# Two-layer hybrid backbone on one core: modulation slices in another order, and the first two feature tiles projected side by side

## The chip, the cores and the metric

The kernel runs on one NeuronCore of a Trainium2 chip. The metric is the device time of one execution in microseconds (us); less is better. All the work is float32 or float32 split into two parts, and the engines run side by side, held together by semaphores that are written out by hand.

## What is computed

Two layers work on 512 latent and 256 context tokens (768 columns here) of width 1024. In each layer a normed and modulated token matrix is projected, four branches mix the tokens, a gated sum is projected back, and a gated feed-forward part follows. Only the first lines of the first layer matter here:

```python
mod_l = (jax.nn.silu(c) @ w_mod[l] + b_mod[l])[:, None, :]
mod_c = (jax.nn.silu(c_ctx) @ w_mod[l] + b_mod[l])[None, None, :]
sh1, sc1, g1, sh2, sc2, g2 = jnp.split(mod_l, 6, axis=-1)
...
hl = modulate(rms_norm(x, norm1[l]), sh1, sc1)
hc = modulate(rms_norm(xc, norm1[l]), sh1c, sc1c)
y_l, y_c = token_mixer(hl, hc, w_in[l], ...)     # zl = split_cols(hl @ w_in), zc = split_cols(hc @ w_in)
```

`modulate(h, shift, scale)` is `h * (1 + scale) + shift`.

## The kernel before

**Operand tiles.** The modulated matrix is held turned, as 8 tiles of 128 features by 768 tokens. Each is split into a leading part `hh` (ScalarE, L1508) and a rest `hl` (VectorE, L1998); weights are split in the same way into `w_hi` and `w_lo` by GpSimd (L1342, L1345). A product is then three matmuls (L517 to L519).

**Modulation.** `w_mod` of the first layer comes as slices of 256 by 512 (`msl`, group g, quarter kk). Group 0 and 1 are the two halves of the shift `sh1`, group 2 and 3 those of the scale `sc1`; groups 4 to 11 are for later. PE multiplies each slice by the conditioning (L614). When a group's four slices are done, ScalarE copies the sum out (`modulation_columns`, L1475), PE turns it (`modulation_turned`, L623) and ScalarE adds the bias (`modulation_bias`, L1480). VectorE makes the factor `a1` of the norm from groups 2 and 3 (L1904). Between the slices PE turns the 8 tiles of normed tokens (`turn_tokens("xn", k)`, L998), which ScalarE (even k, L1417) and VectorE (odd k, L1855) copy to SBUF. Before, the groups come in the order 0, 1, 2, 3, and all 8 operand tiles are made after the last of them.

**The raw tokens.** While the first feature tile is projected, PE also turns the raw tokens (`turn_tokens("x", n)` inside `product`), and ScalarE copies each to `xT` (`tokens_again`, L1417), over the normed tile that has been read by then.

**Feature tiles.** The retention branch has four feature tiles, here called f0 to f3, then two pairs of token tiles. Each feature tile is 8 steps of the contraction by 768 columns, in a run of 512 and one of 256 columns for each half of the contraction. f0 uses PSUM banks 0 and 1, f1 banks 2 and 3, f2 banks 0 and 1 again. The modulation groups 0 to 3 use banks 0 to 3, group 4 uses bank 7, and the turned tokens use banks 4 to 7.

**The ring.** All weights come through a ring of four slots of 512 KB, in the order of `weight_chunks`, on SP's DMA queue. A chunk is issued only when the chunk four places ahead of it has been used (a `msl` slice: by PE; a feature tile: when both halves have been split by GpSimd). Counted from 0, the 16 slices of groups 0 to 3 have the places 0 to 15. Before, f0 has place 16, slices 4.0 and 4.1 have 17 and 18, f1 19, slices 4.2 and 4.3 20 and 21, f2 22, slices 5.0 and 5.1 23 and 24, and f3 25. The tables `dist` and `rope` are issued on the same queue, behind f0 and behind f1.

## Time and profile before

| | us |
|---|---|
| median of 3 runs | 2730.15 |
| lowest and highest of them | 2726.96 and 2737.42 |
| the profiled execution | 2744.37 |
| its span, first to last instruction | 2742.6 |
| PE busy in it | 2596.0 (95%) |
| VectorE, ScalarE, GpSimd busy | 1354.9, 714.2, 1472.9 |

The span is what the instructions cover; 1.8 us of the profiled execution lie around it. The profiled execution took 14.2 us more than the median of the runs, so a step that is read from the trace is worth the same microseconds, but is taken from another total. Busy shares are means over the whole: the first 2% of the span, which the change touches, look quite different from the rest.

### The profile page before, as it was taken

To read this page: it belongs to the slowest core of one execution; us is meant where nothing else is said; L and a number is where in the kernel's file an instruction comes from. 1 tells how busy PE (TensorE), PEld (TensorE's weight loads), DVE (VectorE), ACT (ScalarE), POOL (GpSimd) and SP (SyncE) were. 2 spreads that over 40 slices of the span, in tenths; PEclk is the share of its full clock that TensorE was granted. 3 is DMA by queue.
4 is the path that set the end of the run, shared out by engine and by line. 5 is a ranking of instruction groups with operands and counts; after the bars stand their busy time and mean duration, and the time that the engine had idled before them with its cause. 6 is when DMAs were issued, how large, how long until landed. Compare 5 with 4: busy or idle time off the path is not lost.

```text
span 2742.6 us, 37892 instructions
## 1 busy us (share of the span) xinstructions
PE 2596.0 (95%) x15444; PEld 2141.7 (78%) x15444; DVE 1354.9 (49%) x1877; ACT 714.2 (26%) x1216; POOL 1472.9 (54%) x1375
## 2 busy tenths in 40 slices
PE   5999999998998999999999999998999889999999
PEld 2788887877876888888878888796777667888877
DVE  3522256543466867555574463326653767512231
ACT  4411333222254621111120121133331455211110
POOL 2533547522423436666669435546733436588886
PEclk8999999999999999999999999999999999999999
DMA  7422412311311844444433462312221227433322
GB/s 266 146 72 73 141 43 68 87 43 57 105 42 58 267 122 126 122 121 122 121 102 112 127 215 67 86 51 69 74 62 43 62 74 245 116 100 93 98 85 79
DMA packets 378210, 285.23 MB, mean 104 GB/s; under 512 B 10309, under 2 KB 338729, under 8 KB 377526
## 3 DMA queue, kind: packets, MB, share of 16 engines
q1 hardware_dynamic: 375744, 279.94, 34.2%
q8 instruction: 123, 2.02, 0.3%
q10 hardware_dynamic: 1686, 2.78, 0.3%
q14 instruction: 49, 0.40, 0.0%
q0 software_dynamic: 608, 0.09, 0.0%
HBM read 253.42 MB, written 29.36 MB: 103 GB/s over the span
## 4 chain that ended last, share of the span: by engine, by line
PE 80%; DVE 10%; POOL 3%; ACT 3%; issue 2%; DMA 1%; ACTq 0%; SPq 0%; DVEq 0%; POOLq 0%
PE ps L517 18%; PE ps L518 17%; PE ps L519 17%; PE ps L1191 3%; PE ps L723 3%; PE ps L561 2%; PE ps L563 2%; PE ps L562 2%; DVE ffl L2421 2%; PE ps L807 2%; PE ps L827 1%; POOL w_lo L1345 1%; PE ps L932 1%; POOL w_hi L1342 1%; PE ps L1140 1%
## 5 line engine op out<-in xcount | busy, mean ns | idle before, releaser
L1342 POOL TENSOR_TENSOR w_hi<-ring,tiny 128x512 fp32r<-128x512 f32 x480 | 537.5, 1120 | 1037.8 <-PE ps L519 626.9
L517 PE MATMUL ps<-hh,w_hi 128*128 128x512 f32 (+1 forms) x2320 | 848.4, 366 | 15.8 <-DVE hl L1998 9.5
L1345 POOL TENSOR_TENSOR w_lo<-ring,w_hi 128x512 fp32r<-128x512 f32 (+1 forms) x568 | 796.1, 1404 | 98.3 <-ACT w_hi L1546 60.3
L518 PE MATMUL ps<-hl,w_hi 128*128 128x512 f32 (+1 forms) x2320 | 823.7, 355 | 0.0
L519 PE MATMUL ps<-hh,w_lo 128*128 128x512 f32 (+1 forms) x2320 | 822.7, 355 | 0.0
L517 PEld LDWEIGHTS ps<-hh,w_hi 128*128 128x128 f32 x2320 | 444.6, 192 | 112.2 <-issue 27.2
L519 PEld LDWEIGHTS ps<-hh,w_lo 128*128 128x128 f32 x2320 | 444.5, 192 | 61.9
L518 PEld LDWEIGHTS ps<-hl,w_hi 128*128 128x128 f32 x2320 | 445.0, 192 | 58.5 <-issue 2.4
L1644 ACT ACTIVATE arena<-ps,tiny,vec 128x768 f32<-128x768 f32 (+1 forms) x120 | 108.7, 906 | 192.4 <-DVE tiny L2156 185.9
L2430 DVE SCALAR_TENSOR_TENSOR arena<-ps,vec,arena 128x511 f32<-128x511 f32 x66 | 43.6, 660 | 219.8 <-ACT arena L1810 219.0
L517 PE MATMUL ps<-ffh,w_hi 128*128 128x512 f32 x352 | 139.7, 397 | 12.8 <-DVE ffl L2421 11.4
L1810 ACT ACTIVATE arena<-ps,vec 128x768 f32<-128x768 f32 (+1 forms) x44 | 39.1, 888 | 424.5 <-PE ps L519 424.5
L1921 DVE SCALAR_TENSOR_TENSOR rope<-ring,tiny,rope 128x1024 f32<-128x1024 f32 x84 | 146.0, 1779 | 0.9
L519 PE MATMUL ps<-ffh,w_lo 128*128 128x512 f32 x352 | 137.2, 390 | 0.0
L518 PE MATMUL ps<-ffl,w_hi 128*128 128x512 f32 x352 | 137.1, 390 | 0.0
L561 PE MATMUL ps<-w_hi,hh 128*128 128x256 f32 x448 | 131.6, 294 | 3.7 <-POOL w_lo L1345 2.7
L1526 ACT ACTIVATE arena<-ps 128x512 f32<-128x512 f32 (+3 forms) x118 | 66.8, 568 | 249.6 <-PE ps L519 246.1
L563 PE MATMUL ps<-w_hi,hl 128*128 128x256 f32 x448 | 128.5, 287 | 0.0
L562 PE MATMUL ps<-w_lo,hh 128*128 128x256 f32 x448 | 128.5, 287 | 0.0
L2155 DVE TENSOR_REDUCE tiny<-ps 128x1 f32<-128x768 f32 (+1 forms) x120 | 101.4, 845 | 47.6 <-PE ps L791 30.1
L561 PEld LDWEIGHTS ps<-w_hi,hh 128*128 128x128 f32 x448 | 87.7, 196 | 10.5 <-issue 6.8
L517 PEld LDWEIGHTS ps<-ffh,w_hi 128*128 128x128 f32 x352 | 66.0, 188 | 36.9 <-DVE ffl L2421 15.6
(262 smaller groups left out, 3798.9 us busy)
## 6 DMA issues: line engine op xcount, KB each, us to landing
ring<-in_w_in SPq DMA_DIRECT2D x118, 512.0 KB, 4.0
ring<-in_w_mod SPq DMA_DIRECT2D x96, 512.0 KB, 3.9
ring<-in_w_up SPq DMA_DIRECT2D x88, 512.0 KB, 4.2
ring<-in_w_down SPq DMA_DIRECT2D x48, 512.0 KB, 3.7
ring<-in_w_out SPq DMA_DIRECT2D x32, 512.0 KB, 3.8
logits<-arena SPq DMA_DIRECT2D x32, 384.0 KB, 2.3
arena<-logits SPq DMA_DIRECT2D x32, 384.0 KB, 4.1
ring<-in_w_down SPq DMA_DIRECT2D x24, 384.0 KB, 3.2
```

Of the source, the lines that this page charges most:

```text
L517: pe.matmul(acc, wh[:, offset + k], hi[:, n, x:y], start=n == 0, stop=False)
L518: pe.matmul(acc, wh[:, offset + k], lo[:, n, x:y], start=False, stop=False)
L519: mm = pe.matmul(acc, wl[:, offset + k], hi[:, n, x:y], start=False, stop=n == whole - 1)
L561: pe.matmul(to, hh[:, n, ts], wh[:, :, k], start=n == 0 and bank_begins, stop=False)
L562: pe.matmul(to, hh[:, n, ts], wl[:, :, k], start=False, stop=False)
L563: mm = pe.matmul(to, hl[:, n, ts], wh[:, :, k], start=False, stop=n == KT - 1 and bank_ends)
L723: mm = pe.matmul(psum(("oT", l, b, t))[64 * s:64 * s + 64, P * c:P * c + P], vt, pt[s][:, m], start=m == key_tiles(t)[0], stop=m == NT - 1)
L1342: pool.tensor_tensor(wh[:, 0:count], w, one[:].unsqueeze(2).to_broadcast([P, count, P]), ALU.mult).then_inc(*up("w_lead", ("lead", key, j)))
L1345: pool.tensor_tensor(wl[:, 0:count], w, wh[:, 0:count].bitcast(F32), ALU.subtract).then_inc(*up("w_split", ("split", key, j)))
L1644: act.activation(prob[:, h % 2, m, lo:T], psum(key)[:, lo:T], ACT.Exp, scale=scale, bias=nmx[:, c:c + 1], accum_out=rsum[t % 2][:, 4 * m + ...
L1921: ins = dve.scalar_tensor_tensor(out=mod_sum[:, s], in0=w, scalar=cs[:, s, k:k + 1], in1=mod_sum[:, s], op0=ALU.mult, op1=ALU.add)
L2155: link(dve.tensor_reduce(nmx[:, c:c + 1], acc[:, lo:T], AX, ALU.max))
```

## The change

- **Order of the slices.** `FIRST_GROUPS = (0, 2, 1, 3)`: the first halves of shift and scale come first. A group is turned behind the first slice of the next group, where it stood behind all four of them.
- **Operand tiles.** The factor `a1` is made in halves (`first_scale`). ScalarE and VectorE make operand tiles 0 to 3 after groups 0 and 2, and tiles 4 to 7 after groups 1 and 3. The later copies of normed tokens now stand among them on both engines. The scratch tiles `tb_first` move to another place in SBUF.
- **First two feature tiles.** `opening_pair` projects f0 and f1 together: for each step of the contraction the six matmuls of f0, the six of f1 and the turning of one raw token tile.
- **Ring and queues.** f1 follows f0 at place 17, and slices 4.0 to 4.3 stand behind it at 18 to 21; f2 keeps place 22. The load of `dist` moves from behind f0 to behind f1. GpSimd splits the halves in the order f0 first, f1 first, f0 second, f1 second.

```diff
+FIRST_GROUPS = (0, 2, 1, 3)
+OPENING = [("f", 0, "ret", 0), ("f", 0, "ret", 1)]
...
             for j, n in enumerate(feature_order(b)):
-                order += [("f", l, b, n)] + slices_behind(l, b, j)
+                order += [("f", l, b, n)]
+                if ("f", l, b, n) != OPENING[0]:
+                    order += (slices_behind(l, b, 0) if ("f", l, b, n) == OPENING[1] else []) + slices_behind(l, b, j)
...
-                    for g in range(4):
+                    for i, g in enumerate(FIRST_GROUPS):
                         for kk in range(4):
                             modulation_slices(("msl", l, g, kk))
+                            if kk == 0 and i > 0:
+                                modulation_turned(FIRST_GROUPS[i - 1])
                             if kk % 2 == 1:
-                                turn_tokens("xn", 2 * g + kk // 2)
+                                turn_tokens("xn", 2 * i + kk // 2)
...
-                        if g > 0:
-                            modulation_turned(g - 1)
-                    modulation_turned(3)
+                    modulation_turned(FIRST_GROUPS[3])
...
+                def opening_pair():
+                    for key in OPENING:
+                        next_chunk(key)
+                        for sem, c in room(key, *banks()):
+                            pe.wait_ge(sem, c)
+                    for j in range(2):
+                        for k in range(KT // 2):
+                            n = KT // 2 * j + k
+                            for key in OPENING:
+                                if k == 0:
+                                    pe.wait_ge(*at(("split", key, j)))
+                                for x, y in segs(T):
+                                    mm = product(psum(key)[:, x:y], key, j, hh, hl, x, y, count=1, first=n, offset=k,
+                                                 each=lambda k: ("hl", l, 1, k))
+                                if k == KT // 2 - 1:
+                                    mm.then_inc(*up("pe_half", ("half", key, j), *([("full", key)] if j else [])))
+                            turn_tokens("x", n)
...
+                    if l == 0 and b == "ret":
+                        opening_pair()
+                        behind(b, 0)
...
-                if key == ("f", 0, "ret", 0):
+                if key == ("f", 0, "ret", 1):
                     sp.dma_start(*loads[2]).then_inc(*up("dist_in", ("dist_in",), by=16))
...
+                    modulation_columns(FIRST_GROUPS[0])
+                    decays()
+                    tokens_out("xn", xn, 2)
+                    modulation_bias(FIRST_GROUPS[0])
+                    modulation_columns(FIRST_GROUPS[1])
+                    modulation_bias(FIRST_GROUPS[1])
+                    act.wait_ge(*at(("scale_set", 1, 0)))
+                    for k in range(KT // 2):
+                        act.wait_ge(*at(("free", ("xn", k))))
+                        lead_of(k)
+                        if k == 1:
+                            tokens_out("xn", xn, 4)
+                    modulation_columns(FIRST_GROUPS[2])
+                    modulation_bias(FIRST_GROUPS[2])
+                    tokens_out("xn", xn, 6)
+                    modulation_columns(FIRST_GROUPS[3])
+                    modulation_bias(FIRST_GROUPS[3])
+                    tokens_again(0)
+                    act.wait_ge(*at(("scale_set", 1, 1)))
+                    for k in range(KT // 2, KT):
+                        act.wait_ge(*at(("free", ("xn", k))))
+                        lead_of(k)
+                        tokens_again(k - 3)
+                    for k in range(KT - 3, KT):
+                        tokens_again(k)
```

SP's queue at the opening of the first layer, before: the twelve slices that wait for a slot, f0, `dist`, slices 4.0 and 4.1, f1, `rope`, slices 4.2 and 4.3, f2.

```order
L1269 DMA ring<-in_w_mod 128x2x512 [waits pe_raw] x12
L1269 DMA ring<-in_w_in 128x8x128 [waits pe_raw]
L1276 DMA dist<-in_k_dist 128x896
L1269 DMA ring<-in_w_mod 128x2x512 [waits pe_raw] x2
L1269 DMA ring<-in_w_in 128x8x128 [waits pe_raw]
L1278 DMA rope<-in_k_rope 128x3072
L1269 DMA ring<-in_w_mod 128x2x512 [waits w_split]
L1269 DMA ring<-in_w_mod 128x2x512 [waits pe_raw]
L1269 DMA ring<-in_w_in 128x8x128 [waits pe_raw]
```

The same place of SP's queue in the changed kernel.

```order
L1296 DMA ring<-in_w_mod 128x2x512 [waits pe_raw] x12
L1296 DMA ring<-in_w_in 128x8x128 [waits pe_raw] x2
L1303 DMA dist<-in_k_dist 128x896
L1305 DMA rope<-in_k_rope 128x3072
L1296 DMA ring<-in_w_mod 128x2x512 [waits pe_raw] x2
L1296 DMA ring<-in_w_mod 128x2x512 [waits w_split] x2
L1296 DMA ring<-in_w_in 128x8x128 [waits pe_raw]
```

f0 and f1 are now next to each other, both tables stand behind them, and f2's wait for PE (`pe_raw`) is one for slice 4.0, which PE takes behind the whole pair, where it took it behind f0 alone.

ScalarE, before, from the second group's column copy: L1475 is the column copy, L1480 the bias, L1417 a token copy, L1438 to L1441 the exponentials and the logarithm of `decays`, L1508 the leading part of an operand tile.

```order
L1475 ACTIVATE arena<-ps 128x512
L1438 ACT_TABLE_LOAD
L1438 ACTIVATE tiny<-tiny 128x16
L1439 ACTIVATE tiny<-tiny 128x4
L1441 ACT_TABLE_LOAD
L1441 ACTIVATE tiny<-tiny 128x16
L1417 ACTIVATE xT<-ps 128x768
L1480 ACTIVATE modv<-ps,vec 128x2 x4
L1475 ACTIVATE arena<-ps 128x512
L1417 ACTIVATE xT<-ps 128x768
L1480 ACTIVATE modv<-ps,vec 128x2 x4
L1475 ACTIVATE arena<-ps 128x512
```

ScalarE in the changed kernel, from the second group's column copy on (L1502 is the column copy, L1507 the bias, L1444 a token copy, L1523 the leading part).

```order
L1502 ACTIVATE arena<-ps 128x512
L1507 ACTIVATE modv<-ps,vec 128x2 x4
L1523 ACTIVATE hh<-xT,modv,tiny 128x512
L1523 ACTIVATE hh<-xT,modv,tiny 128x256
L1523 ACTIVATE hh<-xT,modv,tiny 128x512
L1523 ACTIVATE hh<-xT,modv,tiny 128x256
L1444 ACTIVATE xT<-ps 128x768
L1523 ACTIVATE hh<-xT,modv,tiny 128x512
L1523 ACTIVATE hh<-xT,modv,tiny 128x256
L1523 ACTIVATE hh<-xT,modv,tiny 128x512
L1523 ACTIVATE hh<-xT,modv,tiny 128x256
L1502 ACTIVATE arena<-ps 128x512
```

The leading parts of four operand tiles now stand between the second and the third group's column copies, and `decays` has moved ahead of them, behind the first group's.

## Rows read from the trace of the kernel before

**Rows 1.** The page's head.
```profile
span 2742.6 us, 37892 instructions
```

**Rows 2.** Busy time by stretch; then PEclk, the granted clock (1.00 is 2.4 GHz).
```profile
core 0: us, PE busy (x) PEld busy (x) DVE busy (x) ACT busy (x) POOL busy (x), PEclk, DMA share, GB/s
52.10:57.70 5.60, 0.00 (x0) 0.00 (x0) 4.72 (x5) 3.21 (x8) 4.77 (x5) 0.64 1.10 389
57.80:67.30 9.50, 8.31 (x27) 6.30 (x27) 7.74 (x9) 4.00 (x6) 4.96 (x4) 0.50 0.32 126
115.20:118.50 3.30, 3.30 (x17) 3.30 (x17) 3.26 (x3) 0.00 (x0) 3.22 (x3) 0.50 0.51 132
57.70:80.70 23.00, 19.20 (x100) 15.29 (x102) 16.63 (x23) 13.64 (x20) 5.05 (x4) 0.79 0.14 55
81.70:90.30 8.60, 8.60 (x56) 7.46 (x56) 3.89 (x3) 4.60 (x5) 2.53 (x2) 1.00 0.59 183
```

**Rows 3.** Waits from 57 to 92 us: us in total, times, longest us.
```profile
PE ps L517 <- DVE hl L1998: 9.5, 6, 5.7
```

**Rows 4.** Timeline, 36 to 58 us: start, us, engine, line, tiles [idle before <-releaser].
```profile
36.31 0.60 ACT L1475 ACTIVATE arena<-ps 128x512 f32<-128x512 f32 x1 [1.25 <-PE ps L614]
...
43.63 0.60 ACT L1475 ACTIVATE arena<-ps 128x512 f32<-128x512 f32 x1 [1.68 <-PE ps L614]
...
49.61 0.60 ACT L1475 ACTIVATE arena<-ps 128x512 f32<-128x512 f32 x1 [0.41 <-PE ps L614]
...
51.67 1.04 POOL L1342 TENSOR_TENSOR w_hi<-ring,tiny 128x512 fp32r<-128x512 f32 x1 [40.51 <-DMA ring<-in_w_in]
52.09 0.72 ACT L1480 ACTIVATE modv<-ps,vec 128x2 f32<-128x2 f32 x4 [0.17 <-PE ps L623]
52.79 1.26 POOL L1345 TENSOR_TENSOR w_lo<-ring,w_hi 128x512 fp32r<-128x512 f32 x1
52.91 1.17 DVE L1904 SCALAR_TENSOR_TENSOR tiny<-modv,vec 128x16 f32<-128x16 f32 x1 [1.48 <-ACT modv L1480]
...
54.12 2.50 ACT L1508 ACTIVATE hh<-xT,modv,tiny 128x512 fp32r<-128x512 f32 x4 [1.31 <-DVE tiny L1904]
...
57.74 0.77 PE L517 MATMUL ps<-hh,w_hi 128*128 128x512 f32 x1 [5.69 <-DVE hl L1998]
```

**Rows 5.** SP's issues of f0 and f1 in the timeline.
```profile
46.20 0.37 SPq L1269 DMA_DIRECT2D ring<-in_w_in  x1
...
49.60 0.37 SPq L1269 DMA_DIRECT2D ring<-in_w_in  x1
```

**Rows 6.** DMA issue of f1 (window 49.5 to 49.9): KB, us to landing.
```profile
ring<-in_w_in SPq DMA_DIRECT2D x1, 512.0 KB, 7.5
```

**Rows 7.** DMA issue of a w_in chunk on an idle queue (161.0 to 161.5).
```profile
ring<-in_w_in SPq DMA_DIRECT2D x1, 512.0 KB, 3.9
```

**Rows 8.** The chain that ended last, 78 to 92 us: start, us, what.
```profile
78.66 0.66 PE ps L998 x6
...
80.73 1.07 PE ps L614 x8
...
82.17 5.46 DMA ring<-in_w_in
...
87.69 1.77 POOL w_hi L1342
...
89.53 2.02 POOL w_lo L1345
...
91.69 0.47 PE ps L517
```

**Rows 9.** Timeline: the last raw token's copy, and the first token tile's matmul.
```profile
79.43 0.81 ACT L1417 ACTIVATE xT<-ps 128x768 f32<-128x768 f32 x1 [1.24 <-PE ps L998]
...
114.33 0.36 PE L561 MATMUL ps<-w_hi,hh 128*128 128x256 f32 x1 [2.69 <-POOL w_lo L1345]
```

65 lines of the change are left out of this document (29 added, 36 removed).

## The prediction

> **What bounds the kernel now.** I began with the page's head: the span is 2742.6 us [rows 1], and over nearly all of it PE is the bound, with work that the change leaves alone. So all that can be won or lost lies in the opening of the first layer, and I read that stretch in three views. The busy times by stretch show PE idle for 5.6 us, 52.1 to 57.7, and then at the half clock until 67.3 [rows 2]. The waits show for whom: PE waits 9.5 us in six pieces for operand tiles (`hl`), the longest 5.7 us [rows 3]. The timeline shows the chain ahead of that wait: last bias at 52.09, factor `a1` at 52.91, leading parts from 54.12, first product at 57.74 [rows 4]. f0 then takes 23.0 us, while f1, whose tiles are all there, takes 8.6 us with two slices in it [rows 2]. Behind f1 the chain of waits shows the next bound, and it is another one: f2's weights are issued only when PE has used slice 4.0 (80.73 and on), take 5.46 us to land and 3.8 us to split, and f2 starts at 91.69, when f1 had been done for about a microsecond [rows 8]. That DMA is hidden by f1 now. I compare both kernels at the start of f2, since the chunks, slices and waits behind it keep their order.
>
> **The change, part by part.** All times are on the clock of this trace.
>
> *Operand tiles 0 to 3.* The second group's columns are copied at 36.31 [rows 4]; it is now group 2. Turning group 0 behind that group's first slice puts about 0.9 us of PE in front, and breaks a pair of slices that ran together, so I put this copy at 38.1. The turn of group 2 follows one slice of 1.0 us and the turned tile of 0.9 us, and ends near 40.7; bias 0.72 us, and `a1`. L1904 took 1.17 us for 16 columns, from 52.91 to 54.08, just as long as a GpSimd split (52.79 to 54.05) ran beside it [rows 4]; at 41 us GpSimd has nothing to do, so I take 0.2 us, and 1.17 us as the upper end. Leading parts start at 41.8 instead of 54.1. That is 12.3 us of head start, and the question is how much of it reaches PE.
>
> *What stands behind them.* ScalarE needs 2.50 us for two leading parts [rows 4], so four and one token copy (0.81 us, [rows 9]) hold it from 41.8 to 47.6. Only then comes the third group's column copy, which was done at 43.63 [rows 4]. PE wants it for the turn that now stands behind the fourth group's first slice, and waits from about 46.3 to 48.3. That turn (0.9), slice 13 (1.0), a token tile, two slices (1.9), the last token tile, the last column copy (0.60), turn and bias (0.72) follow: slice 13 is used at 50.2, and the last bias ends at 55.4, against 52.8 before. The pair needs this last bias, since f1's bank 3 holds that group's turn. So the head start is eaten up on ScalarE: PE could begin 2.3 us earlier than now, no more.
>
> *f0 and f1.* f0 is issued at 46.3 as before (46.20, [rows 5]) and is split in its first half by 53.5. f1 waits for slice 13, so its issue falls at 50.3, against 49.60 [rows 5]. It landed in 7.5 us with `dist` and two slices in front of it [rows 6]; an idle queue gives 3.9 us [rows 7]. Now only the tail of f0 is in front, and both tables start behind it; I take 4.0, it lands at 54.3, and GpSimd's 1.04 and 1.26 us [rows 4] make its first half ready at 56.8. With 7.5 us it would be 60.2.
>
> *The pair.* At the full clock one step of one feature tile is an eighth of 8.6 less 1.1 us of slices, rounded up 1.04 with its drain [rows 2, 8], and a raw token tile 0.6 to 0.66 us [rows 8]. Eight steps are 8 x (2 x 1.04 + 0.6) = 21.4 us, of which f0's first 1.04 us is done while f1 is being split: 56.8 + 20.4 = 77.2. Tiles 4 to 7 do not hold it up: ScalarE makes tile 4 behind the first raw token copy, at about 60.7, and one more in each 2.7 us, while PE wants tile 4 at 66. GpSimd has split the second halves by 62.
>
> *f2.* Slice 4.0 goes into bank 7, which the last raw token tile has only just left; its copy takes 0.81 us [rows 9]. Before, f0's narrow columns lay between the two. So slices 4.0 and 4.1 run from 78.1 to 79.2, then f2 is issued, first in the queue: 3.9 us [rows 7], 83.1. The split takes 2.3 us alone [rows 4] and 3.8 us beside VectorE [rows 8]; the strips of the decay table start on VectorE at about that time, so I take 3.1. f2 starts at 86.2, against 91.69: 5.5 us won. PE has nothing but slices 4.2 and 4.3 meanwhile and is idle for about 6 us.
>
> *The clock.* After 2.69 us without work [rows 9] PE was at the half clock for 3.3 us of full work, 115.2 to 118.5 [rows 2], which costs 1.7 us. A wait of 6 us at f2, new in this kernel, should bring that once: 5.5 - 1.7 = 3.8 us. The two clock losses before the change, at 57.8 to 67.3, hid behind the making of tiles and cost next to nothing, so none is given back. The Trainium skill, "TensorE: Matmul & The Clock Gate", section "What's actually happening", says that the throttled clock is the default and activity lifts it; by that rule too f2 starts at 1.2 GHz. It speaks against the change, since f0's slow stretch cost little and f2's costs in full; taken at its word it would also slow the pair, which is the second rival below.
>
> *Behind f2* I cost everything at nothing. The wait of 2.69 us at the first token pair [rows 9] hangs on weights issued behind f2's own slices and moves with it. The strips on VectorE begin earlier by about as much as f2. `dist` and `rope` land a few microseconds later or earlier, long before their use.
>
> **The sum.** 2742.6 - 3.8 = 2738.8 us of span. Against the median of the runs, 2730.15, it is 2726.4; I say 2726.5.
>
> **The rivals.**
>
> *No gain, since f1 comes late* (0.15). Both tables follow f1 at once and share its engines; if it takes 7.5 us as before, the pair ends at 80.6, f2 starts at 89.6 and the clock takes 1.7: 0.4 us won, 2729.8. For it: [rows 6]. Against: what slowed f1 there lay in front of it.
>
> *Slower, by the clock* (0.15). PE idles for 2 us at 46.3 and again around 55 and 56; before, an idle stretch at 52 left it at the half clock until 67.3 [rows 2]. If the pair runs at 1.2 GHz as long as that, from 56.8 to 67.3, it does 10.5 us of time in 5.2 of work: end at 82.4, f2 at 91.4, and with twice the loss of [rows 2] there (3.4) the kernel is 3.1 us slower: 2733.3. It decides against the change once the half clock lasts over 7.6 us in the pair. Against: PE is busy in most of the stretch from 48.3 on.
>
> *The whole head start comes through* (0.04). If f2's weights were there when the pair ends, f2 would start at 78.3, 13.4 us earlier: 2716.8. Its issue waits for a slice that PE uses only behind the pair, and nothing in the diff changes that.
>
> *It does not do what it says* (0.04). Were the last bias or a bank the bound even more (ScalarE's leading parts and token copies in a worse order than I laid out), the pair would start at 58 to 60 and the time would be that of before or a microsecond or two above: 2731.
>
> **How the numbers follow.** Forecast 0.62 (its own range 6.5 to 1 us won), the four rivals 0.38. The bounds of the unknown costs: f1's landing 3.4 us, split 0.7 us either way, `a1` 1.0 us, clock 0 to 3.4 us at f2. So the change moves the time from 6.5 us less to 3.5 us more. The three runs lie 3.2 us below to 7.3 us above their median, so a median of new runs may sit a few microseconds off; 2719.5 to 2736 holds all but the ends. A measurement tells about 0.5%, 13.7 us, from no change. Not one case but the third rival reaches near it: within 0.5% 0.93, faster 0.03, slower 0.04, the last for something in the later layers that I have not seen.
>
> **What would show it.** The first `hh` activation near 42 us and not 54 (step one). ScalarE's third column copy near 47.7, with PE idle before the turn that follows. The first product of the pair at 55.5, a wait for a GpSimd split until about 57, and the pair's end at 77 to 80. An issue of f2 near 79, an idle PE of 6 us, f2's first product at 86, at a granted clock of 0.50. From f2 to the first token pair 22.6 us, as now, plus the clock's loss. It is wrong if f1's landing or the clock differs, most likely towards less gain; it is quite wrong if f2 starts right behind the pair.

## The result, and the profile after

| | before | after |
|---|---|---|
| median, us (21 runs each, side by side) | 2733.38 | 2739.30 |
| lowest and highest | 2725.29 and 2744.18 | 2735.65 and 2747.17 |
| span of the profiled execution, us | 2742.6 | 2744.0 |

The ratio after to before is 1.0025, interval 1.0014 to 1.0035: the changed kernel is slower by about 6.8 us (3.8 to 9.6). The forecast was 2726.5 us with a range up to 2736. The time lies above that range, and the change moved it the other way than forecast, if within the 0.5% that the forecast took for no change.

The busy times of the changed kernel by stretch (the columns are those of [rows 2]).

```profile
26.10:39.80 13.70, 12.34 (x45) 5.82 (x49) 3.32 (x7) 4.71 (x8) 0.00 (x0) 0.50 0.43 136
60.20:63.70 3.50, 3.02 (x11) 2.73 (x12) 0.00 (x0) 0.00 (x0) 3.42 (x4) 0.51 0.96 374
86.20:93.90 7.70, 0.02 (x3) 0.04 (x1) 4.14 (x3) 4.62 (x7) 4.13 (x3) 0.81 0.89 272
93.90:97.80 3.90, 3.90 (x9) 3.10 (x10) 3.83 (x3) 0.00 (x0) 3.82 (x3) 0.50 0.00 1
```

Where before PE was idle from 52.1 to 57.7 [rows 2], it is now idle from 86.2 to 93.9, and works at the half clock behind that. Ahead of everything that the change was to speed up, PE is at the half clock from 26.1 to 39.8, where it was from 26.4 to 33.2 before. The waits of the changed kernel from 84 to 150 us (us in total, times, longest) name what PE waited for; before, the longest wait there was the 2.69 us of [rows 9].

```profile
PE ps L523 <- POOL w_lo L1372: 7.7, 1, 7.7
PE ps L565 <- POOL w_lo L1372: 4.0, 1, 4.0
```

The timeline, with the columns of [rows 4]: L618 is a slice, L1502 a column copy, L627 a turn, L1507 a bias, L2036 the factor `a1`, L1523 the leading part, L523 a product.

```profile
32.51 1.92 PE L618 MATMUL ps<-ring,cs_wide 128*32 128x512 f32 x4 [0.92 <-DVE vec L1900]
34.36 1.87 PE L627 MATMUL ps<-tiny,arena 128*128 128x2 f32 x8
36.16 1.92 PE L618 MATMUL ps<-ring,cs_wide 128*32 128x512 f32 x4
...
44.50 0.17 DVE L2036 SCALAR_TENSOR_TENSOR tiny<-modv,vec 128x8 f32<-128x8 f32 x1
44.70 2.51 ACT L1523 ACTIVATE hh<-xT,modv,tiny 128x512 fp32r<-128x512 f32 x4 [0.51 <-DVE tiny L2036]
...
50.20 0.57 ACT L1502 ACTIVATE arena<-ps 128x512 f32<-128x512 f32 x1
...
57.57 0.47 PE L523 MATMUL ps<-hh,w_hi 128*128 128x512 f32 x1 [1.12 <-ACT modv L1507]
...
60.68 0.80 PE L523 MATMUL ps<-hh,w_hi 128*128 128x512 f32 x1 [1.82 <-POOL w_lo L1372]
```

The first leading part stands at 44.70, against 54.12 before [rows 4]: the head start exists, 9.4 us. The first product stands at 57.57, against 57.74: nothing of it reaches PE. What follows is a long pair, and the chain that ended last shows the rest.

```profile
52.90 5.15 DMA ring<-in_w_in
58.12 1.18 POOL w_hi L1369
...
79.90 0.66 PE ps L1002 x6
...
82.65 0.67 PE ps L1002 x6
83.42 0.82 ACT xT L1444
84.29 1.09 PE ps L618 x8
85.38 4.24 DMA ring<-in_w_in
89.69 2.00 POOL w_hi L1369
91.76 2.00 POOL w_lo L1372
93.90 0.77 PE ps L523
...
111.90 1.87 POOL w_hi L1369
113.84 2.00 POOL w_lo L1372
```

The pair ends at 83.3. The copy of the last raw token tile, two slices, f2's DMA and its split then stand one behind the other, each on its own, and f2 starts at 93.90. Before, slice 4.0 stood ahead of f1, so that f2's DMA (5.46 us) and its split ran under f1's 8.6 us, and f2 started at 91.69 [rows 8]. So f2 is 2.2 us later. The first token pair starts at 119.64, against 114.33 [rows 9]: 5.3 us later. That this is near the 6.8 us of the ratio is in part chance: the opening of this execution ran at the half clock for longer than that of the kernel before, and experiments 3 and 9 show that this alone is worth some 3 us at this place.

### The profile page after: what moved, and what is told of

It reads as the page before. It is cut to its first block, busy times and chain, and to the rows that moved or that the text cites. A ratio compares the mean times of both kernels' runs of the same rounds, so it can differ in the third digit from the quotient of the medians.

```text
span 2744.0 us, 37903 instructions
## 1 busy us (share of the span) xinstructions
PE 2594.8 (95%) x15444; PEld 2141.1 (78%) x15444; DVE 1345.3 (49%) x1878; ACT 713.2 (26%) x1216; POOL 1469.4 (54%) x1375
## 4 chain that ended last, share of the span: by engine, by line
PE 81%; DVE 10%; POOL 3%; ACT 2%; DMA 2%; issue 2%; ACTq 0%; DVEq 0%; SPq 0%; POOLq 0%
PE ps L523 18%; PE ps L524 17%; PE ps L525 17%; PE ps L1218 3%; PE ps L727 3%; PE ps L565 2%; PE ps L566 2%; PE ps L567 2%; DVE ffl L2469 2%; PE ps L811 2%; POOL w_lo L1372 2%; PE ps L831 1%; POOL w_hi L1369 1%; PE ps L936 1%; PE ps L1153 1%
## 5 line engine op out<-in xcount | busy, mean ns | idle before, releaser
L523 PE MATMUL ps<-hh,w_hi 128*128 128x512 f32 (+1 forms) x2320 | 850.1, 366 | 15.3 <-POOL w_lo L1372 9.5
L1372 POOL TENSOR_TENSOR w_lo<-ring,w_hi 128x512 fp32r<-128x512 f32 (+1 forms) x568 | 794.6, 1401 | 94.3 <-ACT w_hi L1586 56.2
L525 PE MATMUL ps<-hh,w_lo 128*128 128x512 f32 (+1 forms) x2320 | 822.7, 355 | 0.0
L523 PEld LDWEIGHTS ps<-hh,w_hi 128*128 128x128 f32 x2320 | 445.4, 192 | 109.9 <-issue 29.8
L525 PEld LDWEIGHTS ps<-hh,w_lo 128*128 128x128 f32 x2320 | 445.0, 192 | 62.6
L523 PE MATMUL ps<-ffh,w_hi 128*128 128x512 f32 x352 | 139.7, 397 | 12.8 <-DVE ffl L2469 11.4
L525 PE MATMUL ps<-ffh,w_lo 128*128 128x512 f32 x352 | 137.2, 390 | 0.0
L567 PE MATMUL ps<-w_hi,hl 128*128 128x256 f32 x448 | 129.0, 288 | 0.0
L523 PEld LDWEIGHTS ps<-ffh,w_hi 128*128 128x128 f32 x352 | 66.0, 188 | 37.1 <-DVE ffl L2469 15.8
```

The lines of the kernel that those rows point to most:

```text
L523: pe.matmul(acc, wh[:, offset + k], hi[:, n, x:y], start=n == 0, stop=False)
L525: mm = pe.matmul(acc, wl[:, offset + k], hi[:, n, x:y], start=False, stop=n == whole - 1)
L567: mm = pe.matmul(to, hl[:, n, ts], wh[:, :, k], start=False, stop=n == KT - 1 and bank_ends)
L1372: pool.tensor_tensor(wl[:, 0:count], w, wh[:, 0:count].bitcast(F32), ALU.subtract).then_inc(*up("w_split", ("split", key, j)))
```

## The experiments

Ratios are to the kernel before, with a 95% interval; 0.001 of it is 2.7 us. "Tokens" is the first matmul of the first token pair in the profiled execution, at 114.33 before and at 119.64 in the changed kernel. All these kernels do the whole computation; number 6 does some matmuls more. Where a kernel ran twice, the second line is its second profile and its second ratio.

| kernel | first leading part | f2 issued | tokens | ratio |
|---|---|---|---|---|
| before | 54.1 | 82.2 | 114.3 | 1 |
| after | 44.7 | 85.4 | 119.6 | 1.0025 (1.0014 to 1.0035) |
| 1 early turns alone | 54.5 | 83.3 | 115.5 | 1.0008 (0.9996 to 1.0020) |
| 2 after, late turns | 47.0 | 86.3 | 118.6 | 1.0032 (1.0019 to 1.0046) |
| 3 after without the pair | 41.6 | 74.1 | 106.3 | 0.9986 (0.9973 to 0.9999) |
| 3 again | 45.0 | 77.1 | 109.3 | 0.9985 (0.9975 to 0.9996) |
| 4 pair alone | 52.4 | 85.3 | 119.5 | 1.0024 (1.0009 to 1.0039) |
| 5 after, f2 covered | 41.7 | 64.4 | 110.8 | 1.0000 (0.9987 to 1.0012) |
| 6 after, PE kept busy | 44.8 | 85.3 | 120.0 | 1.0041 (1.0024 to 1.0058) |
| 7 without the pair, late turns | 46.6 | 76.0 | 108.1 | 0.9991 (0.9977 to 1.0004) |
| 8 pair alone, f2 covered | 54.2 | 63.7 | 112.3 | 0.9998 (0.9983 to 1.0013) |
| 9 after, tables later | 41.3 | 83.4 | 115.8 | 1.0024 (1.0014 to 1.0034) |
| 10 without the pair, turns behind the second slice | 42.0 | 73.5 | 105.6 | 0.9979 (0.9968 to 0.9990) |
| 11 as 10, bank free | 41.9 | 72.2 | 104.3 | 0.9965 (0.9951 to 0.9978) |
| 11 again | 41.9 | 70.9 | 103.1 | 0.9953 (0.9936 to 0.9970) |
| 12 after, bank free | 40.3 | 80.8 | 112.8 | 1.0006 (0.9995 to 1.0018) |

**The theories.** The first: the pair leaves f2's weights nothing to hide under, and that hole costs more than the early tiles win. The rival: the opening itself is worse, since the turns break up slices that ran side by side and ScalarE's longer queue holds the later columns up. A third: the hole is cheap, and the half clock behind it is what costs.

### 1 and 2. The turns alone, and all but the turns

The kernel before, with each group turned behind the next group's first slice:

```diff
                         for kk in range(4):
                             modulation_slices(("msl", l, g, kk))
+                            if kk == 0 and g > 0:
+                                modulation_turned(g - 1)
...
-                        if g > 0:
-                            modulation_turned(g - 1)
```

> The kernel before, with one part of the change: a modulation group is turned behind the first slice of the next group, not behind its last. Groups stay in the order 0, 1, 2, 3, f0 and f1 stay apart. Theory 'slices' (the turn breaks up slices that ran side by side and holds PE at the half clock, so the ring's issues come late): f0 is issued near 49.5 us instead of 46.2, f2 starts near 94.5 instead of 91.7, ratio to before 1.001. Theory 'cover' (the loss is f2's DMA, uncovered by the pair): nothing of it is in this kernel, f0's issue within 0.5 us of 46.2, ratio 1.000.

The changed kernel, with the turns back behind all four slices:

```diff
-                            if kk == 0 and i > 0:
-                                modulation_turned(FIRST_GROUPS[i - 1])
...
+                        if i > 0:
+                            modulation_turned(FIRST_GROUPS[i - 1])
```

> The changed kernel, with that one part undone: groups are turned behind their successor's last slice, all else as changed. Theory 'slices': f0's issue is back near 46.2 us (49.6 as changed), f1's product starts near 57 instead of 60.7, f2 near 90 instead of 93.9, and the kernel comes back to 1.000 to 1.001 of before, from 1.0025. Theory 'cover': f2 still waits 7 to 8 us for its weights, ratio at least 1.002.

The turns alone moved the token pair by 1.2 us and the ratio by 0.0008, an interval that takes in 1. Undoing them in the changed kernel gave 1.0032, no better than 1.0025. So where the turns stand explains at most a small part. That leaves other costs of the opening open, and experiment 12 found one.

### 3. Without the pair, twice

Early tiles as in the changed kernel; f0 and f1 one behind the other, with ring, `dist` and splits as before.

```diff
-                order += [("f", l, b, n)]
-                if ("f", l, b, n) != OPENING[0]:
-                    order += (slices_behind(l, b, 0) if ("f", l, b, n) == OPENING[1] else []) + slices_behind(l, b, j)
+                order += [("f", l, b, n)] + slices_behind(l, b, j)
...
-                    if l == 0 and b == "ret":
-                        opening_pair()
-                        behind(b, 0)
-                    for j in range(1 if l == 0 and b == "ret" else 0, nf + lag):
+                    for j in range(nf + lag):
```

> The changed kernel with the pair undone: f0 alone, then slices 4.0 and 4.1, then f1, with the ring's order, the place of the table loads and the splits as before; slice groups and operand tiles as changed. Theory 'cover': f1 hides f2's DMA again; f0 runs from 57.6 to about 72 us, f1 to 80.5, f2 starts near 82 instead of 93.9 (91.7 before), the wait there is under 1 us, ratio to before 0.9965. Theory 'slices': the late ring costs as much as in the changed kernel, so the ratio stays at 1.001 or more.

> The kernel without the pair and with early tiles once more (turn behind the first slice), to narrow its ratio: 0.9986 [0.9973, 0.9999] in five rounds. Theory 'the 8 us that its trace won at the first token pair are worth 8 of 2730': 0.997 to 0.9985. Rival 'they are given back later or were chance': 0.9995 to 1.0005.

Both runs are faster than before, 0.9986 and 0.9985, and faster than the changed kernel by 0.0040, some 11 us. The chain that ended last in the first of them, around f2:

```profile
74.11 5.48 DMA ring<-in_w_in
...
81.48 2.01 POOL w_lo L1368
83.63 0.47 PE ps L521
```

f2 is issued at 74.11 and loads under f1, as before the change; it starts at 83.63, after a gap of 0.39 us on PE. That is 8.1 us sooner than in the kernel before (91.69 in [rows 8]), and 10.3 sooner than in the changed kernel.

The two profiled executions of this one kernel differ by 3.5 us at the first leading part and by 3.0 at the token pair. ScalarE's first leading part and the stretch ahead of it, of the first execution:

```profile
33.30:39.80 6.50, 6.50 (x45) 3.25 (x42) 1.59 (x5) 2.52 (x8) 0.00 (x0) 1.00 0.73 244
...
41.55 2.50 ACT L1519 ACTIVATE hh<-xT,modv,tiny 128x512 fp32r<-128x512 f32 x4 [0.51 <-DVE tiny L2032]
```

And of the second:

```profile
33.30:39.80 6.50, 6.50 (x26) 3.17 (x26) 0.36 (x1) 0.69 (x2) 0.00 (x0) 0.50 0.49 160
...
45.04 2.51 ACT L1519 ACTIVATE hh<-xT,modv,tiny 128x512 fp32r<-128x512 f32 x4 [0.51 <-DVE tiny L2032]
```

The granted clock is 1.00 in one and 0.50 in the other, over the same 6.5 us of the same program: PE is busy all of the time in both, and does 45 instructions or 26. Both had been at the half clock before that, and one came out of it at 32.1, the other at 40.2. So a single trace tells this opening to some 3 us only, and traces are best compared between executions whose opening ran at the same clock.

### 4. The pair alone

The kernel before, with `opening_pair`, the new ring order, `dist` behind f1 and the new order of the splits, and with the groups, turns and tiles of before.

```diff
+                    if l == 0 and b == "ret":
+                        opening_pair()
+                        behind(b, 0)
+                    for j in range(1 if l == 0 and b == "ret" else 0, nf + lag):
```

> The kernel before with the other part alone: f0 and f1 step by step together, with the changed order of the ring, of the table loads and of the splits; slice groups in the order 0, 1, 2, 3, turned as before, all operand tiles behind the last. Theory 'cover': the pair ends near 83 us, PE then waits about 8 us for f2's weights, f2 starts near 93.5, the first token pair near 118, ratio to before 1.002. Theory 'slices': this kernel has the old slices and the pair alone costs nothing, ratio 1.000.

1.0024: as much loss as the whole change has. PE waits as in the changed kernel, first for f2, then for the first token pair:

```profile
93.77 0.77 PE L522 MATMUL ps<-hh,w_hi 128*128 128x512 f32 x1 [7.68 <-POOL w_lo L1371]
...
119.52 0.55 PE L564 MATMUL ps<-w_hi,hh 128*128 128x256 f32 x1 [3.90 <-POOL w_lo L1371]
```

In the changed kernel these two stand at 93.90 and 119.64. Adding the early tiles to it brought nothing: the leading parts come 7.7 us sooner (44.7 against 52.4), yet the pair ends at 83.3 in the one and at 83.2 in the other. But the two ends have different causes. In the pair alone the chain inside the pair runs over the making of operand tiles: PE waits for `hl` again and again (0.47 us at 64.81, 0.57 at 71.16, 0.48 at 77.39). In the changed kernel it runs over PE alone, behind f1's late split. So the equal ends are a coincidence and do not show that the pair swallowed the early tiles; experiment 12 bears on that.

### 5 and 8. f2 covered, with and without the early tiles

Slice 4.3 changes places with f2 in the ring, so that f2 waits for the split of f1 and no longer for a slice that PE takes behind the pair. On PE, slice 4.3 and the turn of its group go behind f2.

```diff
-                if ("f", l, b, n) != OPENING[0]:
-                    order += (slices_behind(l, b, 0) if ("f", l, b, n) == OPENING[1] else []) + slices_behind(l, b, j)
+                if ("f", l, b, n) == OPENING[1]:
+                    order += slices_behind(l, b, 0) + slices_behind(l, b, 1)[:1]
+                elif ("f", l, b, n) != OPENING[0]:
+                    order += (slices_behind(l, b, 1)[1:] if (l, b, j) == (0, "ret", 2) else []) + slices_behind(l, b, j)
```

> The changed kernel with one swap in the ring and on PE: slice 4.3 goes behind f2, so f2 has place 21 and waits for f1's split (about 65 us) instead of slice 4.0 (85.4). Nothing is left out. Theory 'cover': the wait of 7.7 us at f2 goes, f2 starts near 86.5 instead of 93.9, at the full clock; the first token pair comes near 111 instead of 119.6, and the kernel at 0.9995 of before or a little under. Rival 'given back': the time returns at the next chunk (f3 or the token pair, or at the turn of group 4, which now follows its last slice at once), and the ratio stays above 1.001.

> The kernel before with the pair and the same swap of slice 4.3 and f2, slice groups in the order 0 to 3, operand tiles all behind the last group. Beside the changed kernel with that swap it tells what the early tiles are worth once f2 is covered. Without them the pair ended at 83.2 us, with them at 83.3, so f2 should start near 86.5 in both and the ratios agree within 0.001; if the early tiles are worth something that the wait at f2 hid, this kernel is slower by that.

The chain of the covered kernel (here L620 is a slice, L525 a product of f2, L567 the first token pair, L1509 the column copy of group 4):

```profile
83.42 1.91 PE ps L620 x12
85.33 0.43 PE ps L525
...
94.91 0.60 ACT arena L1509
...
110.78 0.55 PE ps L567
```

f2 is issued at 64.42, 21 us sooner, and starts right behind the slices at the full clock. The token pair moves from 119.6 to 110.8, of which some 4 us are the opening's clock, full in this execution: against experiment 9, whose opening ran alike, it is 5.0 us (115.8). The ratio goes from 1.0025 to 1.0000. With the pair alone the same edit takes 1.0024 to 0.9998. Both steps are clear of their noise (6.8 and 7.1 us, give or take 4.5 and 5.8, worked out from the intervals). So closing the hole at f2 gives back the loss. It gives no gain over before. Group 4's column copy stands behind f2 now, at 94.91, the tables of decay behind that on ScalarE and VectorE, and the token pair waits 3.6 us for ScalarE (L1573): a new wait in place of the old one.

### 6. PE kept busy in the hole

Twelve matmuls whose results nobody reads stand between the slices and f2. They are there for the clock alone.

```diff
+                            if b == "ret" and j == 1 and l == 0:
+                                pe.wait_ge(*at(("free", ("x", 6))))
+                                for _ in range(12):
+                                    pe.matmul(ps[:, 2048:2560], ident, small[:, 0:512], start=True, stop=True)
```

> The changed kernel with work added: 12 float32 matmuls of 128x512 into a free bank, whose result nobody reads, behind slice 4.3, where PE waits 7.7 us for f2's weights. They cannot delay f2 and keep PE busy. If the half clock at f2 costs what its rows say (3.9 us of full work at 0.50), f2 to the first token pair takes 1.9 us less (23.8 instead of 25.7 us) and the kernel 0.0005 to 0.0007 less; if the clock is no part of the loss, nothing moves.

The timeline of this kernel, where f2 would have waited:

```profile
86.11 10.14 PE L1091 MATMUL ps<-small 128*128 128x512 f32 x23
...
96.11 0.80 PE L523 MATMUL ps<-hh,w_hi 128*128 128x512 f32 x1
...
119.97 0.36 PE L565 MATMUL ps<-w_hi,hh 128*128 128x256 f32 x1 [3.59 <-POOL w_lo L1376]
```

Each of the twelve matmuls leaves two records. The clock stayed at 1.00, but the filler ran too long: f2's first half was split by 92.7 and f2 started at 96.1, 3.4 us after it could have. From f2's start to the token pair it took 23.9 us, where the changed kernel took 25.7: the 1.9 us less that were forecast for the clock. So f2 is 2.2 us later than in the changed kernel and the token pair only 0.3. The ratio, 1.0041 from seven runs, is not clear of 1.0025 by the intervals and prices neither filler nor clock. On the third theory the trace speaks: the half clock behind the hole is about 2 us, and the hole itself, with 6.7 and 7.7 us of wait where the kernel before had about one, is not cheap.

A second view of the clock's share is the mean granted clock of every timed run. It is 0.9827 over 120 runs of the kernel before, 0.9811, 0.9812 and 0.9809 for three kernels with the open hole (after, 4, 9), and 0.9827 and 0.9830 for the two with f2 covered (5, 8). Among the 120 runs of before the time falls from 2742.0 us at 0.978 to 2726.5 at 0.987, 1.7 us for each 0.001. So 0.0016 less is 2.8 us, an estimate: of the 6.8 us, some 2 to 3 are the clock and some 4 to 5 the wait. It is a loose one. The other kernels with the open hole have 0.9799 (2) and 0.9817 (12), and this one, whose trace has no half clock at f2, has 0.9814.

### 7 and 10. Where the turns stand, without the pair

The kernel of experiment 3, with its turns behind all four slices (7), and behind the second slice of the next group (10):

```diff
-                            if kk == 0 and i > 0:
+                            if kk == 1 and i > 0:
                                 modulation_turned(FIRST_GROUPS[i - 1])
```

> No pair (f0 and f1 apart as before), early operand tiles, and each group turned behind its successor's last slice. Theory 'ring': without the pair the start of f0 is set by its weights (issued at 48.0 and split at 56.4 with the early turns); with late turns f0's issue comes at 46.5 to 47, but the operand tiles come at 47 instead of 41.6 and ScalarE copies the third group's columns only then: f0 starts at 56 to 58, the first token pair at 106 to 108, ratio 0.998 to 0.999. Rival: the early turns carry the gain of the version without the pair, and this one falls back to 1.000.

> The changed kernel without the pair (ring order, place of `dist` and order of the splits as before), and with each group turned behind the second slice of the next group, not the first. Two slices then run side by side again. Theory 'without the pair the early tiles are a gain, and what is left on top is the pair of slices broken up': the first leading part at 42 to 43, f0 issued about 1 us earlier than with the turns behind the first slice (48.0), the first product at 55.5 to 56.5, the first token pair near 106; ratio 0.9985. Rival 'where the turn stands is indifferent': the same milestones as without the pair and with the turn behind the first slice, 0.9986.

0.9991 late, 0.9979 in the middle, 0.9986 and 0.9985 behind the first slice. The intervals overlap, so the order among the three is not shown. The middle one, clearly faster than before, was taken on for experiment 11. In its trace slices run side by side again, f0 is issued at 44.8 and the first product stands at 55.4.

### 9. The tables behind the slices

```diff
-                if key == ("f", 0, "ret", 1):
+                if key == slices_behind(0, "ret", 0)[1]:
                     sp.dma_start(*loads[2]).then_inc(*up("dist_in", ("dist_in",), by=16))
```

and the same for `rope`.

> The changed kernel with one edit: the loads of `dist` and `rope` stand behind slice 4.1 on SP's queue, not directly behind f1. It prices the landing of f1 by itself (5.15 us from issue to landing in the changed kernel, 4.0 in the prediction). Theory 'the tables share the engines with f1': f1 lands in 3.9 to 4.2 us, its first half is split 1.0 us sooner, the pair ends near 82.2, f2's issue moves to 84.3 and the first token pair to 118.5; the ratio stays at 1.002, since the hole at f2 stays as long. Rival 'the pair is bound by something else' (last bias, bank 3): f1 lands sooner and f1's first product stays at 60.7.

f1 took 5.5 us to land, not less than the 5.15 with both tables behind it. So the tables are not what made f1 slow. What did is not shown. That two slices had moved into the tables' place does not explain it: f2, in the changed kernel, had two slices and f3 issued within 1.6 us behind it and landed in 4.24 us. Ahead of f1, though, f0 was still landing, until 53.8 here. The ratio, 1.0024, is that of the changed kernel. This run is of use for another reason: its opening ran at the full clock from 30.8 us on, so it shows the changed order without the long half clock of the first trace. Its chain, and VectorE's first strip (a strip is one of VectorE's steps on the table of decay) beside f2's split:

```profile
47.83 5.92 DMA ring<-in_w_in
...
56.26 1.19 POOL w_hi L1369
57.52 1.28 POOL w_lo L1372
58.85 0.79 PE ps L523
...
82.28 1.09 PE ps L618 x8
83.37 4.23 DMA ring<-in_w_in
87.67 1.05 POOL w_hi L1369
...
87.68 1.98 DVE L2154 SCALAR_TENSOR_TENSOR arena<-dist,arena 128x896 f32<-128x896 f32 x1 [13.02 <-ACT arena L1476]
...
90.92 0.77 PE ps L523
```

The load at 47.83 is f0's. It lands at 53.8, GpSimd splits f0's first half until 56.2 and f1's right behind it, without a wait: f1's weights, landed at 55.3, were there by then. So at the full clock the pair's start hangs on f0's weights and not on f1's.

And the stretch behind f2's start, in the columns of [rows 2]:

```profile
90.90:95.60 4.70, 4.68 (x11) 3.73 (x12) 4.59 (x4) 0.00 (x0) 4.62 (x3) 0.50 0.12 36
```

Against the first execution of experiment 3, whose opening also ran at the full clock, f2 starts 7.3 us later (90.92 and 83.63) and the token pair 9.5 us later (115.78 and 106.30). The difference of 2.2 us is f2's half clock: half of 4.7 us is 2.3. The two executions whose opening ran at 0.50, that of the changed kernel and the second of experiment 3, stand 10.3 us apart at the token pair (119.64 and 109.30). The ratios 1.0025 and 0.9985 stand 11 us apart. Traces at equal clock and times agree on the price of the pair: some 10 us.

### 11 and 12. The wait for bank 2

The kernels with the new group order all have one wait that the kernel before did not have: the first slice of the second group waits 0.92 us for VectorE (`vec`, L1900, at 32.51 in the timeline above). That group is group 2 now and takes PSUM bank 2, in which PE has just turned the third piece of the bias rows; before it was group 1, with bank 1 long free. The edit turns that piece into bank 1.

```diff
             def vectors_turned(i):
-                for s, n in room(("vec", i), i):
+                for s, n in room(("vec", i), 1 if i == 2 else i):
```

In the kernel of experiment 10, twice:

> The kernel without the pair and with the turns behind the second slice, with one edit: the third pair of bias rows (`vec`, 2) is turned into PSUM bank 1 and not bank 2, so that the second group's first slice does not wait for VectorE to copy it out (0.92 us of idle PE at 32.5 in the changed kernel, new against before). Theory 'that idle is what keeps PE at the half clock until 36 to 40 in some executions': the profile shows the slice at 31.5 without a wait, the half clock ends at 33.2 or earlier, and the ratio falls from 0.9979 by up to 0.001 (some executions lose 3 us now). Rival 'only the wait itself counts': the first leading part comes 0.5 to 1 us sooner, or not at all if the slices' own DMAs are then waited for, and the ratio stays within 0.0004 of 0.9979.

> The kernel without the pair, turns behind the second slice, bank free, once more, to narrow its ratio of 0.9965 (0.9951 to 0.9978). Theory 'the idle at 31.6 kept PE at the half clock in some executions': 0.996 to 0.997, and its trace has the half clock end before 34. Rival 'only the 0.9 us of wait count': 0.9972 to 0.998, nearer to the 0.9979 of the kernel with the bank not free.

In the changed kernel:

> The changed kernel with the one edit that its second group's first slice waits for no bank: the third pair of bias rows is turned into bank 1 and not bank 2. Theory 'the opening is a second, smaller part of the loss': PE no longer idles for 0.92 us at 31.6 to 32.5, fewer executions stay at the half clock to 36 or 40, and the ratio goes from 1.0025 to 1.001 to 1.0017, the same step as the kernel without the pair made. Rival 'with the pair there the early tiles are covered anyway': as when the turns were put back, nothing of it reaches f2 and the ratio stays at 1.0025.

The one edit takes the changed kernel from 1.0025 to 1.0006, and the kernel of experiment 10 from 0.9979 to 0.9965 and 0.9953. In the first that is 5 us, in the second 4 and 7, for 0.9 us of wait. By the intervals these are 5.2 us give or take 4.3, 3.8 give or take 4.8, and 7.1 give or take 5.5 (estimates; the last two share one comparison kernel). All three go the same way and two are clear of noise, so that the wait costs something is shown; that it costs more than its own 0.9 us is likely, and how much more is open. PE's timeline and the chain of the changed kernel with its bank free:

```profile
31.24 1.05 PE L618 MATMUL ps<-ring,cs_wide 128*32 128x512 f32 x4
...
46.96 4.75 DMA ring<-in_w_in
...
88.32 0.77 PE ps L523
...
112.81 0.49 PE ps L565
```

The slice stands at 31.24 without a wait. Against the execution of experiment 9, whose opening ran at the same clock (and whose tables are loaded later), it is 1.2 us sooner (31.24 for 32.42), f0 is issued 0.9 sooner (46.96 for 47.83) and lands in 4.75 us where it took 5.92, f2 starts 2.6 sooner (88.32 for 90.92) and the token pair 3.0 (112.81 for 115.78). So 3 of the 5 us are followed step by step, 1.2 of them a load of f0 that landed faster, for which no run shows the reason. The mean granted clock of all runs rose from 0.9811 to 0.9817, about 1 us by the relation above, and within its scatter. The theory asked for more than that: in 5 of the 9 profiled executions of kernels with the new group order and the wait, the half clock of the opening lasted until 36 to 40. In the other four it ended by 32.1, and in the seven of kernels without the wait (three with the bank free, four with the old group order) by 33.5. That fits the theory and does not show it.

With the bank free the early tiles are worth something beside the pair too: 1.0006 against the 1.0024 of the pair alone, some 5 us, and 112.8 against 119.5 at the token pair. By the intervals the 4.9 us are uncertain by 5.2, so this gain is likely and not shown. The wait for bank 2 had cost about what they brought. And experiment 11, early tiles without pair and wait, is the fastest kernel of this study: 0.9965 and 0.9953, some 9.5 and 13 us under before, and 16 to 20 under the changed kernel.

## Why the prediction was wrong, point by point

**What bounds the kernel** was read rightly behind the pair, and not ahead of it, as the paragraph on the pair's start tells. The hole at f2 was foreseen in its mechanism, its place and about its size: 6 us forecast, 6.7 and 7.7 measured. So was the half clock behind it, 1.7 us forecast, 2.0 and 2.3 measured. By the Trainium skill, "TensorE: Matmul & The Clock Gate", section "What's actually happening", the throttled clock is the default, so f2 would start throttled; the trace agrees, at 0.50 from 93.90 on.

**The operand tiles** were right where the clock was that of the forecast: the first leading part was put at 41.8 and came at 41.3 in experiment 9 and at 41.6 in the first run of experiment 3. In the changed kernel's own trace it came at 44.7. There the half clock lasted from 26.1 to 39.8 (before: to 33.2), and a turn and a slice took 1.87 and 1.92 us, at 34.36 and 36.16. A wait was overlooked here: the forecast let the second group's slices follow at once, and asked of no bank but bank 3 whether it was free. Group 2's first slice waited 0.92 us for bank 2, and without that wait the ratio is 5 us better (experiment 12; 4 and 7 in experiment 11). The cost of `a1`, 0.2 us with GpSimd at rest, was right (0.17).

**What stands behind them** was right in kind: PE waited for ScalarE's third column copy, put at 47.7, measured 50.20, and the last bias, put at 55.4, ended at 57.2. That is the same 2 to 3 us of clock: in experiment 9 they stood at 46.77 and 54.15.

**The pair's start** was the first term that was too small. f1's first half was to be ready at 56.8 and was used from 58.85 (experiment 9) or 60.68 (the changed kernel), and the two have different causes. In experiment 9 it is f0. The forecast had f0 issued at 46.3 and its first half split by 53.5, and took this for no bound; the kernel before had that half split only by 54.05, from an issue at 46.20 [rows 4, 5]. In experiment 9 the issue came at 47.83, the load took 5.92 us, and the half was split by 56.2. PE, whose last bias was done at 54.15, waited 3.1 us for that, and f1's split could only follow. So the head start of the tiles ran into f0's weights, which the forecast had not moved. In the changed kernel's own trace it is f1: issued at 52.90 for 50.3, since its slice 13 came late with the clock, and landed in 5.15 us for 4.0. The first rival, f1 late, was near this in its number (60.2); its reason, the tables, was not borne out, since f1 took 5.5 us with the tables moved away.

**The pair** was to take 20.4 us behind that. Measured in experiment 9 were 22.5 us, from 58.85 to 81.3, and in the changed kernel 22.6, from 60.68 to 83.3. Two terms are in that: a step of the contraction took 2.76 us and not 2.68 (token turns at 79.90 and 82.65 in the chain of the changed kernel), which makes 0.6 over eight steps, and the first 2.7 to 3.0 us ran at the half clock (60.20:63.70 above), which costs 1.3 to 1.5. The forecast had priced a clock loss at f2 only, and had put the one in the pair into a rival with a chance of 0.15. That rival named the right sign and nearly the pair's end (82.4), but by a half clock of 10.5 us where 3 were measured, so its nearness is luck.

**f2** was right from the pair's end on: 2.0 us to its issue, measured 2.1; 3.9 us of DMA, measured 4.2; 3.1 us of split, measured 3.3 in experiment 9 and 4.2 in the changed kernel, where the first GpSimd piece took 2.00 us and not 1.05. VectorE's first strip began together with it in both, and one of the two engines took twice its time, in the changed kernel GpSimd and in experiment 9 VectorE (the last section).

The sum, for the execution of experiment 9: the pair's start 2.1, the half clock in the pair 1.3, the steps 0.6, f2's DMA, split and issue 0.6 make 4.6 of the 4.7 us by which f2 was late (90.9 for 86.2). With 0.6 more of half clock, the token pair stood at 115.8 and not at 110.5.

**Behind f2 all at nothing.** "From f2 to the first token pair 22.6 us plus the clock's loss" held in experiment 9: 24.9 us, 2.3 of it clock. In the changed kernel it was 25.7, and 1.2 us came from a term that the forecast had at nothing: the first token tile's weights were split in 1.87 and 2.00 us, at 111.90 and 113.84, beside VectorE's strips, where the kernel before had the same two pieces done in 1.04 and 1.30, since VectorE's first strip began only at 109.78:

```profile
107.86 1.04 POOL L1342 TENSOR_TENSOR w_hi<-ring,tiny 128x512 fp32r<-128x512 f32 x1 [4.69 <-DMA ring<-in_w_in]
108.97 1.30 POOL L1345 TENSOR_TENSOR w_lo<-ring,w_hi 128x512 fp32r<-128x512 f32 x1
```

**The step that failed** is thus the sum up to the pair's end: 77.2 us forecast, 81.3 measured at the full clock and 83.3 in the changed kernel's own trace. Two of its terms had been put at nothing, the half clock in the pair (left to a rival) and the wait for bank 2, and one path, that over f0's weights, was taken for no bound. f2 was forecast 5.5 us early, and terms of 1 to 2 us, each put at its better end, ate that up. With the overlooked wait taken out, experiment 12 measured 1.0006 (0.9995 to 1.0018), no gain shown, where 3.8 us (0.9986) were forecast. The range of the change allowed it to be 3.5 us slower, while the pair's start, the clock in the pair and the splits beside VectorE all fell to the bad side at once, and of the overlooked wait it had nothing.

**In sum**, by the ratios: the pair costs 6.6 us alone (experiment 4) and 10.9 beside the early tiles (after and experiment 3). The early tiles with the bank free bring about 5 us beside the pair (12 and 4), which the intervals do not quite show. The wait for bank 2 takes about 5 us back (12 and after). Each of these is uncertain by some 4 to 5 us. What stays open is a part of the last: 2 of its 5 us are in no trace. A trace and a ratio agree on differences of such kernels to 2 or 3 us, and less well against before: experiment 5 beat before's trace by 3.5 us at the token pair with a ratio of 1.0000, and no second trace of before was taken.

**What was not seen** is a comparison the rows allowed: before, f1's 8.6 us, with two slices in them, were the cover of f2's DMA and split, which take 9.5 us together [rows 8]. Any order that uses f1 up before f2 is issued pays for these in full. The forecast knew the hole and priced it in full, and set it against a head start that it had itself cut from 12.3 to 2.3 us.

## What to carry to other kernels

Before two stretches of work are run together, ask what each was the cover of: here the ring frees f2's slot by a slice that PE took between f0 and f1, and together they leave 4.2 us of DMA and 3 to 4 us of split with nothing to run under. A change of several parts is worth measuring in parts; the early tiles were good, the pair bad, and a wait for a PSUM bank that neither needs hid the one behind the other. When groups change their order, list for each the bank or slot it now takes and who held it last: 0.9 us of wait early in a chain cost 3 us by the traces and about 5 by the ratio.

## What the runs showed of the hardware

- The granted clock of one stretch differs between executions of one program: 1.00 and 0.50 over 33.3 to 39.8 in the two runs of experiment 3, with PE busy for all of it. In both PE had idled for 1.5 us before 24.4 and for 0.92 us before 32.7, but the clock had not fallen at the same time: the turns from 24.4 on took 0.48 us each in the first, and in the second 0.33 us until 26 and 0.47 from 27 on. In the first it was back at full by 32.1, in the second at 40.2. What decides it is open.
- The time of a run goes with its mean granted clock: the 120 runs of the kernel before took 2742.0 us at 0.978 (2 runs), 2734.9 at 0.982 (18) and 2726.5 at 0.987 (4). So do profiled spans: 2742.6 us at 0.978 for before, and 2722.1 at 0.987 in experiment 8, whose ratio is 0.9998. Spans of single executions do not rank kernels that differ by 0.3%.
- Two slices side by side take as long as one alone. At the half clock, the eight matmuls of two took 1.94 us, the four of one 1.92 (at 32.51 and 36.16, shown above):

```profile
27.89 1.94 PE L618 MATMUL ps<-ring,cs_wide 128*32 128x512 f32 x8
```

- VectorE's `a1` on a few columns took 0.17 us at 44.50 with GpSimd at rest, 1.17 us on 16 columns beside a split in the kernel before [rows 4], and 0.69 us beside one in experiment 9. The split pays too: the leading part takes 1.04 us alone (111.90 in the chain shows 1.87 beside the strips), the rest 1.30 (113.84 shows 2.00).
- Which of the two pays differed between two executions in which both began within 0.01 us of each other. In experiment 9 GpSimd's piece began at 87.67 and took 1.05 us, and VectorE's strip, at 87.68, took 1.98. In the changed kernel both began at 89.69; there the piece took 2.00 us and the same strip 1.09:

```profile
89.69 1.09 DVE L2154 SCALAR_TENSOR_TENSOR arena<-dist,arena 128x896 f32<-128x896 f32 x1 [13.02 <-ACT arena L1476]
```
